# A layer's three stages as one program per engine, on shared buffer areas

## What is computed

```python
for l in range(DEPTH):                                   # DEPTH = 2
    x = x + 0.5 * swiglu(rmsnorm(x, ffn1_norm[l]), ...)  # 1024 -> 2816 -> 1024
    h = rmsnorm(x, mix_norm[l])
    z = h @ w_in[l]                                      # 4 branches and 4 x 1024 gates
    ...                                                  # convolutions, two attentions
    merged = sum(sigmoid(gate_b) * branch_b)
    x = x + merged @ w_out[l]
    x = x + 0.5 * swiglu(rmsnorm(x, ffn2_norm[l]), ...)
```

## Time and profile before

| | |
|---|---|
| median of 3 runs | 2682.45 us (2682.3 to 2684.92) |
| the profiled execution | 2684.33 us, its span 2682.1 us |
| PE | busy 2493.1 us, 93% of the span |
| PE weight loads | 1664.0 us, 62% |
| DVE | 1212.1 us, 45% |
| ACT | 858.4 us, 32% |
| POOL | 28.2 us, 1% |
| transfers | 687.31 MB, 256 GB/s over the span |
| 0.5 MB piece, issue to landing (median) | 3.4 us (w_mix), 5.1 us (feed-forward) |
| 2 MB expert piece, issue to landing (median) | 20.5 to 25.6 us |

### The profile page before, as it was taken

One profiled execution on the slowest core, in us unless ns is written; L12 is line 12 of the kernel. 1 busy time (PEld: TensorE's weight loads), 2 busy tenths in 40 slices (PEclk: granted clock), 3 DMA queues, 4 the chain that ended last, 5 costly groups with the idle time before them and its releaser, 6 DMA issues. The chain is left out here.

```text
span 2682.1 us, 33027 instructions
## 1 busy us (share of the span) xinstructions
PE 2493.1 (93%) x12876; PEld 1664.0 (62%) x12877; DVE 1212.1 (45%) x1963; ACT 858.4 (32%) x1390; POOL 28.2 (1%) x57
## 2 busy tenths in 40 slices
PE   7998999899899899989979999799999999999997
PEld 6787888688688789868867788333333333333332
DVE  5555756665565575666554465522112112211212
ACT  5344454444344545444444444201001000100101
POOL 0000000000000000000000000000000000000000
PEclk9999999899899999989999999799999999999999
DMA  8754444664674434366452124799999999999985
GB/s 317 251 176 144 130 137 132 235 235 157 225 246 157 150 126 142 126 237 235 156 166 70 65 87 126 325 429 430 427 429 428 428 430 427 429 428 428 430 350 203
DMA packets 113468, 687.31 MB, mean 256 GB/s; under 512 B 20673, under 2 KB 22097, under 8 KB 87793
## 3 DMA queue, kind: packets, MB, share of 16 engines
q1 hardware_dynamic: 105840, 656.47, 63.4%
q0 software_dynamic: 7520, 29.37, 3.1%
q10 hardware_dynamic: 2, 0.01, 0.0%
HBM read 683.70 MB, written 2.11 MB: 256 GB/s over the span
## 5 line engine op out<-in xcount | busy, mean ns | idle before, releaser
L2172 PE MATMUL ps<-wexp_all_second,con_all_whole 128*64 128x512 f32 x3168 | 707.3, 596 | 29.0 <-DMA wexp_all_second<-in_w_lin 28.5
L2172 PEld LDWEIGHTS ps<-wexp_all_second,con_all_whole 128*64 128x64 f32 x3168 | 221.1, 137 | 470.7 <-issue 397.3
L514 DVE TENSOR_TENSOR lo_first<-raw_first,hi_first 128x1024 fp32r<-128x1024 f32 x264 | 308.0, 1220 | 35.4 <-ACT hi_first L471 35.4
L244 PE MATMUL ps<-hi_first,h_hi_first 128*128 128x512 f32 x704 | 285.2, 405 | 23.2 <-DVE lo_first L514 23.2
L245 PE MATMUL ps<-lo_first,h_hi_first 128*128 128x512 f32 x704 | 280.3, 398 | 0.0
L246 PE MATMUL ps<-hi_first,h_lo_first 128*128 128x512 f32 x704 | 280.0, 398 | 0.0
L471 ACT CAST hi_first<-raw_first 128x1024 fp32r<-128x1024 f32 x264 | 259.8, 1054 | 13.5 <-DMA raw_first<-in_ffn_wgu 13.5
L244 PE MATMUL ps<-h_hi_first,w_hi_first 128*128 128x256 f32 x848 | 246.2, 290 | 4.4 <-DVE w_lo_first L975 4.1
L246 PE MATMUL ps<-h_hi_first,w_lo_first 128*128 128x256 f32 x848 | 238.7, 281 | 0.0
L245 PE MATMUL ps<-h_lo_first,w_hi_first 128*128 128x256 f32 x848 | 238.4, 281 | 0.0
L975 DVE TENSOR_TENSOR w_lo_first<-raw_first,w_hi_first 128x1024 fp32r<-128x1024 f32 x122 | 148.6, 1222 | 151.7 <-ACT w_hi_first L886 151.0
(11 more groups left out here) (436 smaller groups left out, 3336.3 us busy)
## 6 DMA issues: line engine op xcount, KB each, us to landing
wexp_all_second<-in_w_gate SPq DMA_DIRECT2D x64, 2048.0 KB, 23.0
wexp_all_second<-in_w_lin SPq DMA_DIRECT2D x64, 2048.0 KB, 25.6
wexp_all_second<-in_w_down SPq DMA_DIRECT2D x64, 2048.0 KB, 20.5
raw_first<-in_ffn_wgu SPq DMA_DIRECT2D x176, 512.0 KB, 5.1
raw_first<-in_w_mix SPq DMA_DIRECT2D x138, 512.0 KB, 3.4
raw_first<-in_ffn_wd SPq DMA_DIRECT2D x88, 512.0 KB, 5.1
raw_second<-in_w_mix SPq DMA_DIRECT2D x57, 512.0 KB, 3.4
wada_first<-in_w_ada POOLq DMA_DIRECT2D x48, 512.0 KB, 5.6
```

The source lines that it names most:

```text
L244: nc.tensor.matmul(out, w_hi, x_hi, start=start, stop=False, skip_group_check=True)
L514: nc.vector.tensor_tensor(lo[:, slot], raw[:, slot], hi[:, slot].bitcast(F32), ALU.subtract).then_inc(s[f"{kind}_lo"], 1)
L2172: mm = nc.tensor.matmul(dst[side(half), :], lhs(k), B.wexp[2 * "gld".index(kind) + part][:, k % 4, half * HALF:(half + 1) * HALF], start=( ...
```

## The change

The three stages of a layer become one phase (`layer_phase`), with 'ffn1.', 'mix.' and 'ffn2.' in front of their semaphores' names. `ffn_stage` and `mixer_stage` give back the parts of each engine, and one program per engine runs them in a row. All buffers of the three stages lie in one fixed arrangement, so that what one stage writes early is free in the stage before: the mixer's weight slots lie over the condition rows, the first feed-forward weights over the mixer's z and gates. Waits between the stages are written out.

- The mixer's loads follow the feed-forward stage's, after the condition sums are copied, which now happens in group 5. Its first two splits come ahead of the x adds.
- x is added, squared, normed and turned by token tile; tile 1's scaling is split between ACT and DVE.
- In the mixer's output product SP loads the next stage's four first pieces ahead of piece 64; ACT and DVE split each one behind an output piece.
- x is turned into banks 2, 3, 6, 7. In the second feed-forward stage squares come behind the activations' halves, not before.
- The expert stage begins with nine matmuls whose result nobody reads.

```diff
-    x_bank = lambda b: ps[:, b, :]
+    x_bank = lambda b: ps[:, (2, 3, 6, 7)[b], :]
...
+    def x_there(eng, t):
+        if first:
+            eng.wait_ge(s[f"x_in{t}"], 16)
+        elif before:
+            before["x"](eng, t)
...
+    def on_pool(pool):
+        if before:
+            before["weights_used"](pool)
+        ada_pool(pool, nc, s, B, l, w_ada, which, first)
...
+        if not before:
+            load(sp, "gu", 0)
...
+        for k in range(KD):
+            halves_act(act, nc, s, x_bank, gain, B.h_hi, k)
+        if before:
+            x_there(act, 0)
+            square_sums(nc, s, B, x[:, 0, :], 0, 1)
+        else:
             upper("gu", 0)
...
+            if 2 * i < ADA_STEPS <= 2 * i + 2:
+                ada_store(dve, nc, s, B, l, which)
...
+    def on_sync(sp, after):
+        before["weights_free"](sp)
+        for c in range(N_MIX):
+            if c == N_MERGE + RAW:
+
+                sp.wait_ge(s["merged"], KD)
+                sp.wait_ge(s["prod"], KD)
+                after.load_first(sp)
...
+        turn_pe(nc, s, B, B.xs, x_bank, lambda t: pe.wait_ge(s[f"x_scaled{t}"], t + 1))
...
+        for t in range(TC):
+            before["x"](act, t)
+            if t:
+                act.wait_ge(s["squared"], t)
+            square_sums(nc, s, B, B.x[:, t, :], t, t)
+            rstd_act(act, nc, s, B, slice(t, t + 1), t + 1)
+        act.wait_ge(s["rstd_ready"], 2)
+        nc.scalar.activation(B.xs[:, 1, 0:HALF], B.x[:, 1, 0:HALF], ACT.Identity, scale=B.stats[:, 3, 1:2]).then_inc(s["x_scaled1"], 1)
...
+        for c in range(N_MERGE + SPLIT, N_MIX):
+            upper(c)
+            if c > N_MERGE + SPLIT:
+                after.upper_first(act, c - N_MERGE - SPLIT - 1)
...
+        before["add_x"](dve, 0, 0)
+        before["add_x"](dve, 0, 1)
+        dve.wait_ge(s["squared"], 1)
+        nc.vector.tensor_scalar(B.stats[:, 1, 0:1], B.stats[:, 0, 0:1], 1.0 / D, EPS, ALU.mult, ALU.add).then_inc(s["var_ready"], 1)
+        before["add_x"](dve, 1, 0)
+        dve.wait_ge(s["std_ready"], 1)
+        nc.vector.reciprocal(B.stats[:, 3, 0:1], B.stats[:, 2, 0:1]).then_inc(s["rstd_ready"], 1)
+        before["add_x"](dve, 1, 1)
+        dve.wait_ge(s["rstd_ready"], 1)
+        before["x"](dve, 1)
+        nc.vector.tensor_scalar(B.xs[:, 0, :], B.x[:, 0, :], B.stats[:, 3, 0:1], None, ALU.mult).then_inc(s["x_scaled0"], 1)
+        rstd_dve(dve, nc, s, B, slice(1, 2), 2, 2)
+        dve.wait_ge(s["rstd_ready"], 2)
+        nc.vector.tensor_scalar(B.xs[:, 1, HALF:], B.x[:, 1, HALF:], B.stats[:, 3, 1:2], None, ALU.mult).then_inc(s["x_scaled1"], 1)
...
+        for c in range(N_MERGE + SPLIT - 1, N_MIX):
+            lower(c)
+            if c > N_MERGE + SPLIT:
+                after.lower_first(dve, c - N_MERGE - SPLIT - 1)
...
+    B.z, B.gates, B.raw = alloc(nc, ctx, B, z=(P, ZC, T), gates=(P, GC, T), raw=(P, RAW, D))
+    B.w_hi, B.w_lo = alloc(nc, ctx, B, F32R, w_hi=(P, SPLIT, D), w_lo=(P, SPLIT, D))
...
+    B.xs = B.gates[:, 4:12, :].rearrange("p (t k) c -> p t (k c)", t=TC)
...
+    with phase(nc, " ".join(names)) as (block, s):
+        of = lambda stage: {n.split(".")[1]: sem for n, sem in s.items() if n.startswith(stage + ".")}
+        s1, sm, s2 = of("ffn1"), of("mix"), of("ffn2")
...
+        mix = mixer_stage(nc, B, sm, l, I["w_mix"], v("mix"), before=dict(
+            x=lambda eng, t: eng.wait_ge(s1["x_done"], 2 * t + 2), add_x=ffn1.add_x,
+            weights_free=lambda sp: sp.wait_ge(s1["a_copied"], 2)))
+        ffn2 = ffn_stage(nc, B, s2, l, 1, I["ffn2_wgu"], I["ffn2_wd"], I["w_ada"], v("ffn2"), before=dict(
+            x=lambda eng, t: eng.wait_ge(sm["x_done"], 2 * t + 2),
+            weights_used=lambda pool: pool.wait_ge(sm["acc_done"], TC)))
...
+        @block.vector
+        def _(dve):
+            ffn1.dve(dve)
+            for c in range(2):
+                mix.lower_first(dve, c)
+            mix.dve(dve, ffn2)
+            ffn2.dve(dve)
...
+            for n in range(WARM):
+                nc.tensor.matmul(h_bank(1, 1), con("ident"), con("before")[:, 0, :], start=True, stop=True)
```

More of the change, by code:

```diff
@@ new lines, in x_there, with upper_unit @@
+    def x_there(eng, t):
[3 more added lines that the diff above has]
+            before["x"](eng, t)
+    def upper_unit(act, kind, i, q):
+        slot = slot_of(kind, i, q)
+        act.wait_ge(s[f"w{slot}"], 16 * loads_before(kind, i))
+        if kind == "d" and i == last_group:
+            act.wait_ge(s["gu_used"], 4 * i + q + 1)
+        elif i > 0:
+            act.wait_ge(s[f"{kind}_used"], UNITS[kind] * (i - 1) + q + 1)
+        nc.scalar.copy(hi[slot], raw[slot]).then_inc(s[f"{kind}_hi"], 1)
@@ new lines, in lower_unit, with add_x @@
+    def lower_unit(dve, kind, i, q):
+        slot = slot_of(kind, i, q)
+        dve.wait_ge(s[f"{kind}_hi"], UNITS[kind] * i + q + 1)
+        nc.vector.tensor_tensor(lo[slot], raw[slot], hi[slot].bitcast(F32), ALU.subtract).then_inc(s[f"{kind}_lo"], 1)
+    def add_x(dve, t, half):
+        dve.wait_ge(s["acc_done"], t + 1)
+        part = x[:, t, half * HALF:(half + 1) * HALF]
+        nc.vector.scalar_tensor_tensor(part, acc[t][half], 0.5, part, ALU.mult, ALU.add).then_inc(s["x_done"], 1)
@@ new lines, in on_pool, with load @@
+    def on_pool(pool):
+        if before:
+            before["weights_used"](pool)
+        ada_pool(pool, nc, s, B, l, w_ada, which, first)
+    def load(sp, kind, i):
+        n = UNITS[kind]
+        for q in range(n):
+            slot = slot_of(kind, i, q)
+            if kind == "d" and i == last_group:
+                sp.wait_ge(s["gu_lo"], 4 * i + q + 1)
+            elif i > 0:
+                sp.wait_ge(s[f"{kind}_lo"], n * (i - 1) + q + 1)
+            src = wgu[l, i, q] if kind == "gu" else wd[l, 2 * i + q]
+            sp.dma_start(raw[slot], src).then_inc(s[f"w{slot}"], 16)
@@ L721, in mixer_program @@
     n_units = 4 * TC * 2
-    rows = "w0 w1 w2 w3 hi lo mm out "
-    names = (NORM + Attention.SEMS + rows + "qk_sq qk_ms qk_var qk_std qk_rstd qk_spread v_turned v_copied sig chain "
+    att = Attention(nc, B, s, mixer_units(nc, B), T,
+                    (lambda u: ps[:, 2 + u % 2, :], lambda u: ps[:, 4, :], lambda u: ps[:, 6 + u % 2, :]))
+    acc = [[ps[:, (6, 0)[t] + half, :] for half in range(2)] for t in range(TC)]
+    prod_bank = lambda c, b: ps[:, 2 + (c % 2) * 2 + b // 2, (b % 2) * T:(b % 2 + 1) * T]
```

1264 lines of the change are left out of this document (620 added, 644 removed).

## The result

The changed kernel takes 2657.53 us (median; 2656.93 to 2660.18), the kernel before 2682.44 on the same chip. The ratio is 0.9905, with a 95% interval of 0.9893 to 0.9916: 25 us less. The profiled execution took 2657.36 us with a span of 2655.5, at 2682.1 before. All medians here are of fast executions: of the six of e1 two took 2881.86 and 6432.81 us and are left out.

What follows compares the result with a forecast made beforehand. Matmul engine bounds the kernel before the expert stage, the weight stream bounds that stage. Joint one 10.3, joint two 16.6 and warm-up 4 sum to 30.9 us: 2682.45 - 30.9 = 2651.5, own range 2645 to 2657, whole range 2640 to 2664.

Steps and rivals of the forecast that it cites:

- Joint one, first product: Feed-forward one to mixer: the mixer's first product comes 6.4 us earlier in layer 0, 5.3 us in layer 1.
- Unit 1's wait: Joint one, mixer's second unit waiting for its weight split's lower half: 0.9 us saved by splitting ahead.
- Joint one, clock: Start of the mixer: new matmul gaps lower the clock, costing 1.6 us a layer; bounds nothing and 2.3 us.
- Joint two, first product: Mixer to feed-forward two: feed-forward two's first product comes 6.6 us earlier in each layer.
- Joint two, clock: Start of feed-forward two: no gap over 1.5 us left, half-rate stretch goes, 2.2 us saved a layer.
- The late row: Mixer's output product: row 64 arrives late behind 2 MB of new loads; 0.5 us cost taken for each layer.
- the rival with 2663: Joint two: output rows 64 to 67 come 6.4 us late in both layers, 11.8 us less saved; chance 0.09.
- The warm-up: Start of expert stage: nine matmuls raise the clock, router's matmuls get shorter, 4 us saved; bounds nothing and some 10.
- The rival by the Trainium skill's rule: Expert stage: warm engine stays warm through the router, whole 10 us come; in the clock-up-everywhere rival, 2641 us, chance 0.13.
- The rivals** "slower": First block's mixer: clock stays low through it, units take 5.1 in place of 2.7 us; 2728 us, chance 0.04.
- "no change": Expert stage: something outside the joints sets its start, so the change does not bite; 2682 us, chance 0.03.
- The signs named ahead: Joints, row 64 and expert stage: trace signs; stage start moved under 22 us makes joints wrong, unchanged 37.7 us the warm-up.

Runs made afterwards that it cites:

- e1: The changed kernel without its nine warm-up matmuls; 2666.4 us, ratio 0.9930.
- e10: The changed kernel with the mixer's first two weight splits moved back to where they stood, behind the norm and the activations' halves; 2661.32 us, ratio 0.9922.
- e9: The changed kernel once more, unchanged, run on one chip beside three further variants; 2659.77 us, ratio 0.9911.
- e5: The kernel before with an unused 576-byte buffer a partition ahead of the mixer's raw weights; 2688.73 us, ratio 1.0014.
- e3: The changed kernel with output row 64 loaded first, then rows 65 to 67 alternating with feed-forward two's four pieces; 2655.35 us, ratio 0.9891.
- e2: The kernel before with the nine warm-up matmuls added and nothing else; 2678.86 us, ratio 0.9983.
- e8: The changed kernel with row 64 loaded first and the mixer's weights moved by 576 bytes; 2652.42 us, ratio 0.9876.
- e12: The changed kernel with row 64 first, weights moved by 576 bytes, and two more idle matmuls in the expert stage; 2645.92 us, ratio 0.9859.
- e11: The changed kernel with row 64 loaded first and the mixer's weights moved by 1024 bytes in place of 576; 2654.68 us, ratio 0.9889.
- e6: The changed kernel with 576 unused bytes a partition between the mixer's raw weights and w_hi; 2653.29 us, ratio 0.9887.

## Why the prediction was right, point by point

The median lies 6 us above the forecast and 0.5 us above its own range (2645 to 2657), but inside the whole range. The places of the gain were right; that the sum came so near is in part luck, as the last paragraph of this section adds up.

- **Joint one, first product** (6.4 and 5.3 us sooner): measured 6.7 and 6.0. The step order was right, with barrier and table load among what shortened, and tile 1's chain ends last. Unit 1's wait of 0.9 is gone in both, but e10 shows that in layer 0 the adds could begin some 2 us sooner without the splits that remove it, where I took 0.5 for them.
- **Joint one, clock** (1.6 us each): a lottery, not a constant. From unit 0's first product to the copy of its result it takes 3.34 us in layer 0 of after and 3.73 in layer 1, so nothing and 0.4 us were paid; in e9, the same kernel, layer 1 takes 4.95 (clock 0.50 from 882 to 886), 1.6 us more. The size was right, that it always comes was not.
- **The mixer's units** were taken as unchanged, without a reason. They lost 2.0 and 3.4 us in the two layers between unit 1 and the output product. This term is missing from the sum. Place explains about 4 us in both layers together (e5); the number of stretches at the low clock differs too, and how the two share the loss in each layer was not told apart. The output product gained 0.5 us in each layer by place (23.45 us from its first to its last product before, 22.92 in e5). The prediction read 0.22 us for 512 columns out of 45 records in 5 us; that counts records which overlap the window's ends, and the starts are 0.1178 us apart, 0.236 for 512 columns. It changes the sum by some 0.2 us.
- **Joint two, first product** (6.6 each): without the late row, e3 saves 6.9 and 7.2 from the first output product to the first product of feed-forward two. Right: 2.65 of it came with the barrier and the order of tiles, 3.8 and 4.1 with the splits, 0.5 with the output product's spacing.
- **Joint two, clock** (2.2 each): right. From the first product to the first silu feed-forward two takes 12.5 us in both layers, before: 14.7 and 14.4, so 2.2 and 1.9 us, and that lead holds up to the last group. The fall behind the gap between groups 0 and 1 stands in both kernels (504 to 507.5 before, 493.7 to 497 after) and cancels out. But whole stages are only 1.4 and 1.2 us shorter, because the joint behind each, whose barrier the change kept, grew by 0.8 and 0.7: in layer 0 the matmul engine stands idle 3.27 us ahead of the next layer's transposes, 2.46 before. That term is missing from the sum too. That the larger phase has more semaphores to clear there may be the cause; no run shows it.

```profile
683.11 1.06 PE L221 MATMUL ps<-con_all_whole,x_whole 128*128 128x128 f32 x8 [2.46 <-PEq L167]
...
673.25 0.95 PE L222 MATMUL ps<-con_all_whole,x_whole 128*128 128x128 f32 x7 [3.27 <-PEq L168]
```

- **The late row** (0.5 each): 4.3 and 1.4 measured by e3. This is the term that was mis-sized, by 4.7 us. The step that failed is the transfer: I let five pieces take 8 us from the first issue to row 64's landing, at the full rate, with 1.9 us for issue and landing. They took 10.1. In its first three windows of 2 us the queue moved 139, 248 and 305 GB/s, which leaves it 2.8 us behind 429 GB/s. I also priced the wait alone, not the fall of the clock behind it (some 1.6 us in layer 0). The upper bound (6.4) was too high, so the rival with 2663 did not come either, but it had the right mechanism.
- **The warm-up** (4): 6.4 in this execution, about 4.4 or 6.6 in others (e1, e2). That the router's matmuls halve was right (1.97 us for 16 records at clock 1.00, 3.62 before). The rival by the Trainium skill's rule ("TensorE: Matmul & The Clock Gate", The HAM clock gate), that a warm engine stays warm, holds only in part: the engine fell back behind small matmuls and waits in after and in e8, and stayed up in e12, where those waits are filled.
- **The rivals** "slower" and "no change": no mixer of the first block stayed at the low clock for more than 7 us at a time in any trace, and what was saved ahead of the expert stage moved its start one for one.
- **The signs named ahead.** Came: the mixer's first product 4.5 us after the last add, feed-forward two's 1.7 us after it, the router at clock 1.00. Did not come: clock 1.00 through joint two (it fell at 463.0, ahead of it), a wait of under 1 us for row 64 (2.34 and 1.11), a stage start moved by at least 22 us (20.2). By the last, which was to make the joints wrong, they were short: they gave 20.1 us in place of 26.9. The gate weights came at 29.05 us, sooner than the 34 named.

The sum was right to 6 us because what went against it (late row 4.7, units 5.4, the joints between the stages that kept their barrier 1.5) met what went for it (joint one's first products and its clock, unit 1 included, 4.2; joint two's first products 1.0; warm-up 2.4). That leaves a saving 4.4 us short of the forecast in the traces; most of the rest is that the profiled execution before lay 1.9 us above its median.

## What to carry to other kernels

When loads for the next stage are put ahead in a queue, ask which piece is needed first by the stage that still runs, and put that one ahead of them; 2 MB in front of one row cost 5.7 us in the traces, and interleaving in the order of use gave it back. Fill the matmul engine's unavoidable waits at the head of a stage with short idle matmuls, and read the granted clock to see whether they hold it. When buffers are moved, compare the start-to-start time of an unchanged loop: place alone can move it, and here it was worst where both operands lay at one place modulo 1024 bytes.

## What the runs showed of the hardware

- The start-to-start time of fp32 matmuls of 256 columns depends on where their operands lie in a partition, at full clock: 0.1200 us wherever both lie at one place modulo 1024 bytes (288 in after, e3, e5 and e11, 704 in the second block of every kernel), 0.1178 or 0.1133 where they differ (736 before, 864 in e6, e8 and e12). What chooses between these two stayed open. For 512 columns it is 0.227 at one place, 0.233 with w at 736 and 0.229 at 864.
- Behind a gap of 2.3 to 2.7 us of the matmul engine the clock sometimes falls, sometimes not. The gap of 2.6 us ahead of unit 28 in the mixer is in every kernel and layer; in before's layer 0 nothing follows (clock 1.00 from 324 to 332), in its layer 1 some 15 products start at double spacing, near 2 us lost. Another fall has no such gap ahead of it, in layer 0 of all kernels but e2: before it stands from 292.4, just behind 14 matmuls on 14 rows, 3.25 us from 288.19. What decides whether a gap is followed by a fall stayed open, and so did how much of the scatter between executions comes from it. The Trainium skill ("TensorE: Matmul & The Clock Gate", What's actually happening) says that how many matmuls run cold at a kernel's start varies from run to run with the same kernel. The traces show the like inside a kernel: in layer 1, behind joint one, e9 paid 1.6 us and after 0.4.
- A queue that starts behind a pause comes to its full rate late: 139, 248, 305 and then 418 GB/s in windows of 2 us from 449 in after, while its eight issues took from 448.98 to 453.87.
